# Keys' chain, branch statistic, token turns and spatial products at other places in the last two layers of a one-core network

## The reference, cut to what matters

```python
for l in range(DEPTH):                                    # DEPTH = 2
    h = rmsnorm_2(x, pre_g[l])
    proj = jnp.einsum('bsd,de->bse', h, w_in[l])
    u_a, v_a, g_a, q, k, v, g_b = jnp.split(proj, idx, axis=-1)
    y_a = gmlp_group(u_a, v_a, ...) * jax.nn.silu(g_a)    # layernorm of v_a, then ws @ vn, + sb, * u
    y_b = gqa_axial_attention(q, k, v, ...) * jax.nn.silu(g_b)  # rmsnorm per head, rope, softmax
    y = jnp.concatenate([y_a, y_b], axis=-1)
    out = jnp.einsum('bse,ed->bsd', y, w_out[l])
    x = x + rmsnorm_2(out, post_g[l])
```

## Time and profile before

| | |
|---|---|
| device time, median of 3 runs | 1638.35 us (1638.33 to 1639.24) |
| profiled execution | 1638.61 us |
| its span | 1636.8 us |
| PE busy | 1599.8 us (98% of the span) |
| DVE busy | 895.1 us (55%) |
| ACT busy | 730.7 us (45%) |
| POOL busy | 713.4 us (44%) |
| first of the two layers, about | 1189 to 1405 us |
| second, about | 1407 to 1630 us |

### The profile page before, as it was taken

One profiled execution on the slowest core, in us unless ns is written; L12 is line 12 of the kernel. 1 busy time (PEld: TensorE's weight loads), 2 busy tenths in 40 slices (PEclk: granted clock), 3 DMA queues, 4 the chain that ended last, 5 costly groups with the idle time before them and its releaser, 6 DMA issues.

```text
span 1636.8 us, 23565 instructions
## 1 busy us (share of the span) xinstructions
PE 1599.8 (98%) x8404; PEld 1266.5 (77%) x8404; DVE 895.1 (55%) x1475; ACT 730.7 (45%) x1155; POOL 713.4 (44%) x406
## 2 busy tenths in 40 slices
PE   8999999999999999999999999999999999999998
PEld 7656688888888887676788888888887777887776
DVE  7787545455431123545266766621176754687665
ACT  6433544443442235444355555533335643445542
POOL 4433244444444544444444444455444543335531
PEclk9999999999999999999999999999999999999999
DMA  7211133233333332111223333243331554324541
GB/s 251 72 53 55 52 115 92 89 101 103 95 99 115 103 103 69 61 52 39 85 76 97 103 103 90 90 127 95 120 115 52 163 137 126 97 81 117 152 140 52
DMA packets 52972, 161.01 MB, mean 98 GB/s; under 512 B 8736, under 2 KB 8864, under 8 KB 52896
## 3 DMA queue, kind: packets, MB, share of 16 engines
q1 hardware_dynamic: 51744, 156.31, 31.5%
q10 hardware_dynamic: 1152, 3.67, 0.7%
HBM read 141.08 MB, written 2.10 MB: 87 GB/s over the span
## 4 chain that ended last, share of the span: by engine, by line
PE 81%; DVE 9%; SPq 3%; ACT 3%; issue 2%; DMA 1%; POOL 1%; DVEq 0%; ACTq 0%; POOLq 0%
PE banks L1887 22%; PE banks L1889 22%; PE banks L1888 22%; SPq L625 3%; PE banks L1933 2%; PE banks L1934 2%; PE banks L1935 2%; PE banks L2159 1%; PE banks L2074 1%; PE banks L2089 1%; PE banks L2106 1%; PE banks L2443 1%; DVE roped L1677 1%; DVE chain L1496 1%; ACT prob_c L799 1%
## 5 line engine op out<-in xcount | busy, mean ns | idle before, releaser
L649 POOL TENSOR_TENSOR w_lo<-raw,w_hi 128x1024 fp32r<-128x1024 f32 x252 | 609.6, 2428 | 695.6 <-ACT w_hi L732 694.6
L1887 PE MATMUL banks<-xs_hi,w_hi 128*128 128x512 f32 (+2 forms) x1488 | 590.4, 397 | 4.1 <-DVE xs_lo L1558 1.6
L1889 PE MATMUL banks<-xs_hi,w_lo 128*128 128x512 f32 (+2 forms) x1488 | 577.0, 388 | 0.0
L1888 PE MATMUL banks<-xs_lo,w_hi 128*128 128x512 f32 (+2 forms) x1488 | 576.5, 387 | 0.0
L732 ACT ACTIVATE w_hi<-raw 128x1024 fp32r<-128x1024 f32 x255 | 263.7, 1052 | 234.9 <-PE banks L1889 199.1
L1887 PEld LDWEIGHTS banks<-xs_hi,w_hi 128*128 128x128 f32 x1488 | 280.2, 188 | 71.7 <-issue 16.3
L1889 PEld LDWEIGHTS banks<-xs_hi,w_lo 128*128 128x128 f32 x1488 | 279.9, 188 | 57.6
L1888 PEld LDWEIGHTS banks<-xs_lo,w_hi 128*128 128x128 f32 x1488 | 280.5, 188 | 52.3 <-issue 0.5
L1889 PE MATMUL banks<-hid_hi,w_lo 128*128 128x512 f32 x352 | 137.0, 389 | 0.0
L1888 PE MATMUL banks<-hid_lo,w_hi 128*128 128x512 f32 x352 | 137.0, 389 | 0.0
L1887 PE MATMUL banks<-hid_hi,w_hi 128*128 128x512 f32 x352 | 137.0, 389 | 0.0
(11 more groups left out here) (270 smaller groups left out, 2017.0 us busy)
## 6 DMA issues: line engine op xcount, KB each, us to landing
raw<-wstream SPq DMA_DIRECT2D x255, 512.0 KB, 3.5
swap_c<-prob_c SPq DMA_DIRECT2D x256, 64.0 KB, 2.0
x<-xT SPq DMA_DIRECT2D x4, 512.0 KB, 10.4
out<-pt SPq DMA_DIRECT2D x8, 256.0 KB, 2.0
memx<-memT SPq DMA_DIRECT2D x4, 256.0 KB, 5.4
ws_sb<-wsT ACTq DMA_DIRECT2D x2, 512.0 KB, 4.6
rope_sb<-rope ACTq DMA_DIRECT2D x2, 512.0 KB, 6.4
qk<-post_rows ACTq DMA_DIRECT2D x2, 512.0 KB, 4.1
```

Of the source, the lines that this page charges most:

```text
L649: nc.gpsimd.tensor_tensor(w_lo[s][:].rearrange("p k c -> p (k c)"), raw[s][:], w_hi[s][:].rearrange("p k c -> p (k c)").bitcast(f32), SUB) ...
L1887: MM(dst, w_hi[slot][:, k, :], hi, start=start, stop=False)
L1888: MM(dst, w_hi[slot][:, k, :], lo, start=False, stop=False)
L1889: return MM(dst, w_lo[slot][:, k, :], hi, start=False, stop=stop)
```

## The change

The same operations are issued in another order. On PE: `key_cast` goes from unit 7 step 5 to step 1, and `keys_up` from step 2 to step 3; `stat("ln")` from unit 13 step 2 to step 5; `to_tokens(0)` from unit 16 step 1 to step 3; `spatial(0)` from unit 18 step 4 to step 3, `spatial(1)` stays at the border of units 18 and 19, `spatial(2)` from unit 19 step 3 to step 5, `spatial(3)` from the end of unit 19 to unit 20 step 1. On DVE: `rope(4)` goes ahead of `invert("qk")`, `key_norm` and `k_low` go up, and in round 19 `mixed(2)` goes behind `maxima`. ACT, POOL and SP keep their order. Both layers are changed alike.

```diff
@@ DVE @@
                     for n, (_, i) in enumerate(steps_in(j)):
                         if j == 18 and n == 1:
                             mixed(0)
+                        if i < a.n:
+                            maxima(a, i)
                         if j == 19:
                             mixed(2)
-                        if i < a.n:
-                            maxima(a, i)
...
                     if j == 6:
                         rope(3)
+                        rope(4)
                         invert(f"qk{l}")
-                        rope(4)
-                    if j == 8:
-                        k_low()
-                    if j == 7:
-                        key_norm()
...
                     if j == 6:
+                        key_norm()
                         q_low(0)
+                    if j == 7:
+                        k_low()
@@ PE @@
                 HEADS_AT = {
                     6: [(t + 1, lambda t=t: head_stats(t)) for t in range(5)],
-                    7: [(2, keys_up), (5, lambda: key_cast())],
+                    7: [(1, lambda: key_cast()), (3, keys_up)],
                 }
...
                     if j == 13:
-                        before.append((2, lambda: stat(f"ln{l}")))
+                        before.append((5, lambda: stat(f"ln{l}")))
...
                     if j == 16:
-                        before += [(1, lambda: to_tokens(0)), (7, lambda: to_tokens(1))]
+                        before += [(3, lambda: to_tokens(0)), (7, lambda: to_tokens(1))]
...
                     if j == 18:
-                        before.append((4, lambda: spatial(0)))
+                        before.append((3, lambda: spatial(0)))
                     if j == 19:
-                        before.append((3, lambda: spatial(2)))
+                        before += [(0, lambda: spatial(1)), (5, lambda: spatial(2))]
+                    if j == 20:
+                        before.append((1, lambda: spatial(3)))
                     unit(u0 + j, a0 + j, before=before, freed=xs_free if j == IN2_UNITS - 1 else None)
                     if j == 17:
                         to_tokens(3)
-                    if j == 18:
-                        spatial(1)
-                    if j == 19:
-                        spatial(3)
```

## The result

The changed kernel takes 1640.56 us, the median of 20 executions (1639.22 to 1642.37). The kernel before, beside it on the same chip, has 1638.35 us as the median of 20 (1637.66 to 1639.52). The ratio is 1.0013, with a 95% interval from 1.0007 to 1.0019. That is 2.2 us or 0.13% longer: within the 0.2% that the prediction calls the same, and inside its range.

What follows compares the result with a forecast made beforehand. PE, busy 98% of the span, was taken as the bound. 6.66 - 2.54 - 2.74 - 3.02 = -1.64 us gave 1636.7; 1.6 to 3.2 us for the clock led to 1639.0, range 1636.2 to 1641.8.

Steps and rivals of the forecast that it cites:

- The new wait: Unit 7: `key_cast` waits for `stat_inv`, made 2.82 us later by `rope(4)`; 3.33 us lost per layer, together 6.66.
- POOL and the shared ports: `rope(4)` on DVE ends ahead of POOL's low part, taking 2.77 us; losing the ports would add up to 2.4 per layer.
- the rival that ends slower: `invert("qk")`'s twelve small operations wait for POOL's low part, 2 us more per layer; with low clock 1643.1 us; chance 0.07.
- What the chain gives back: Units 7 and 8: earlier `key_norm` and `k_low` remove waits at the turns of x and scores; gain 2.54 us.
- Statistic and token turn: Units 13 and 16: one chain, `s_act` stands still; gain 1.37 us per layer, together 2.74, bounds 1.6 and 3.4.
- the sign that the prediction had named: ACT's `token_norm` would end as long after unit 9's first scores as before.
- Spatial product: Unit 19: `spatial(2)` at step 5 no longer waits for `mixed(1)`; gain 1.51 us per layer, 3.02 together.
- DVE's later transposes: Round 19: `mixed(2)` holds transposes and `inverses` some 2 us; costed at nothing, 2 us if the cover were gone.
- the sum (1636.7): Whole kernel without any fall of the clock: 6.66 - 2.54 - 2.74 - 3.02 = -1.64 us, off the median; chance 0.22.
- The clock: Behind the `key_cast` waits: 1.2 GHz for 3.4 us, 1.6 us each, once or twice, 1.6 to 3.2 us.
- its own mechanism: `key_cast` waits and the clock falls once or twice: 1638.3 to 1639.9 us, taken as 1639.0; chance 0.57.
- a stall elsewhere: DVE's late transposes or a moved `s_act` stall PE: 1 to 3 us more, 1640 to 1642 us; chance 0.09.

Runs made afterwards that it cites:

- the two kernels whose `key_cast` is at step 5: Changed kernel with `key_cast` at unit 7 step 5: with DVE's `rope(4)` order and `keys_up` also as before, 1632.93 us; with `key_cast` alone put back, 1630.58 us.
- the statistic alone: Kernel before with only `stat("ln")` moved from unit 13 step 2 to step 5; 1638.09 us, ratio 0.9998.
- the filled kernel: Changed kernel with 14 extra 128x512 matmuls ahead of `key_cast` in unit 7 of each layer, into a bank nobody reads; 1637.10 us, ratio 0.9992.
- the kernel without the chain: Changed kernel with `rope(4)` behind `invert("qk")`, `key_cast` at step 5, `keys_up` at step 2 and `key_norm`, `k_low` as before; 1632.93 us, ratio 0.9968.
- the kernel with the chain alone: Kernel before with only `rope(4)` ahead of `invert`, `key_norm` and `k_low` earlier, `key_cast` at step 1, `keys_up` at step 3; 1645.48 us, ratio 1.0047.
- A wait of 1.9 us: Changed kernel with `key_cast` at unit 7 step 3, ahead of `keys_up`; median 1636.19 us of eleven executions, profiled execution 1634.44 us.

## Why the prediction was right, point by point

**The new wait** was the large term and it came as worked out: 3.33 us predicted, 3.33 measured, twice. Both sides of it were right: the last of the roots ended at 1231.87, 2.65 us later than in the earlier trace rows with PE 0.2 us earlier at the start of the unit (2.82 was predicted), and `key_cast` would have started 0.32 us behind the third matmul.

**POOL and the shared ports.** `rope(4)`'s last operation started at 1228.43 and took 0.69 us, so it ended 0.02 us ahead of POOL's low part at 1229.14, and the small operations under POOL kept their step of 0.24 us. So the 2.13 us of the earlier trace rows did not come back, and the rival that ends slower (1643.1) fell. The two did not overlap here, so this place doesn't test who keeps the ports. The prediction says that the trace has only the case in which POOL started first; it has the other one too, earlier in the same layer of the kernel before:

```profile
1218.97 0.69 DVE L1677 TENSOR_TENSOR roped<-roped,rope_sb 128x512 f32<-128x512 f32 x1
1219.58 2.86 DVE L1678 TENSOR_TENSOR qk<-qk,rope_sb 128x512 f32<-128x512 f32 x1
1219.32 2.58 POOL L649 TENSOR_TENSOR w_lo<-raw,w_hi 128x1024 fp32r<-128x1024 f32 x1 [3.03 <-ACT w_hi L732]
```

The operation that VectorE had started ahead of POOL kept its 0.69 us and POOL took 2.58 instead of 2.40; the next one, started under POOL, took 2.86. The Trainium skill (SBUF — State Buffer, "Who interferes with whom") lets the one that starts first keep the ports; these rows agree, with 0.69 where VectorE started first and 2.86, or 2.13 in the earlier trace rows, where POOL did.

**What the chain gives back**, 2.54 predicted: 2.35 by the two kernels whose `key_cast` is at step 5 (1632.93 - 1630.58).

**Statistic and token turn.** Predicted 2.74, with 1.6 and 3.4 as ends, because `s_act` would stand still. Measured 1.35 and 1.36, together 2.71. That the two waits are one is shown by the statistic alone (0.2 us, where its own wait is 1.8) and by the start of `token_norm`, 0.07 us apart. In the changed kernel it is this row:

```profile
1303.44 2.93 ACT L1048 ACTIVATE va<-va,par 128x512 f32<-128x512 f32 x4
```

It ends 57.98 us after the first `scores` of unit 9 (1248.39), and 57.93 us after them in the kernel before (1301.62 and 1243.69), which is the sign that the prediction had named. The prediction left "about 0.1 to 0.3" at the token turn; it is 0.3 idle, or 0.48 from start to start.

**Spatial product.** Predicted 1.51 in each layer, measured 1.49. No kernel moved it alone; the number is from the traces, and the kernel without the chain (5.5 us faster) has room for it. The later `mixed(2)` cost nothing to see.

**A term that was missing.** I had looked for stalls behind DVE's later transposes and found none. But `weigh` in unit 16 waits 0.2 us in each layer, since PE reaches it earlier and `gated` on DVE doesn't move. It follows from the same argument that I made for the token turn: I asked there what stands still when PE comes earlier, and did not ask it of the next step of PE that hangs on that chain. The timeline of the changed kernel shows it without a bracket, so only the starts tell:

```profile
1308.31 0.40 PE L2069 MATMUL banks<-k_lo,q_stack 128*128 128x512 f32 x1
1308.84 1.52 PE L2442 MATMUL banks<-pt_c,vtok 128*64 128x256 f32 x12
```

They are 0.53 us apart and not 0.32. Twice that is 0.4 us, and the filled kernel (1637.10) lies 0.4 above the sum (1636.7).

**The clock** is the term that was mis-sized. "So I expect the fall to 1.2 GHz behind at least one of the two waits, perhaps both: 1.6 to 3.2 us." It fell at both waits in both kernels that were profiled with them, four times of four, and cost 3.5 us between the medians of the changed kernel and the filled one, 4.1 in the profiled execution. The step that failed in it is the length: I took 3.4 us of low clock from the earlier trace rows for each fall, and one lasted 6.8. The forecast came out at 1639.0 and the median at 1640.56: 0.4 of the difference is `weigh`, the rest is the clock, 3.5 in place of the 2.3 that the forecast had on its sum. So 1640.56 lies above the 1638.3 to 1639.9 that the prediction gave its own mechanism, and inside the time that it gave to a stall elsewhere (1640 to 1642). The traces decide between the two: of such a stall they show the 0.4 us at `weigh` and no more. That the total is inside the stated range owes something to the room that was left for that stall.

**A count.** The prediction speaks of seven named waits with two lines that occur once in each layer. The earlier trace rows has three such lines and three single waits, nine in all. Its sum of 8.9 us counts all nine, so no number hangs on this.

## What to carry to other kernels

When a step of PE is moved to an earlier place, compare the time at which its operand's semaphore rises with the time at which PE gets there, each with its own engine's new order; here the operand became later and the place earlier, and both were the same edit. The two new waits of 3.3 us on TensorE cost about one and a half times their length here (6.66 us and 3.5 for the clock), and matmuls into a free bank took away the clock's third of that price. Waits in a row that hang on one chain of another engine are one wait: moving the first uncovers the second, and the sum over the list of waits is an upper bound, not a gain: here 3.4 us of waits at the statistic and the token turn gave 2.7.

## What the hardware did that I had not expected

- The low clock lasted 6.8 us once and 3.4 us once at two waits that were alike (3.27 us idle in the first layer, 3.29 in the second), in the same execution, and 3.4 us both times in the kernel with the chain alone. The price was 2.7 and 1.4 us in the one kernel, 2.9 for both in the other. The Trainium skill (TensorE: Matmul & The Clock Gate, "Wait — 56ns, not 53.3ns?") gives 426.7 ns between two matmuls of this width at the low clock and 215.7 at the high one; the traces show 0.43 and 0.23 us.
- A wait of 1.9 us left the granted clock at 1.00 in the one execution that was profiled, and the eleven times of that kernel are spread over 4.3 us, where eleven of the filled kernel are spread over 1.2.
- Fourteen matmuls in each layer that nobody needs made the kernel 3.5 us faster than the same kernel without them.
